# A residual kept in the buffer that the expert scatter adds to, and the second product's evacuation on VectorE

## The reference

```python
x = x + gt1 * (merged @ w_out)
h2 = rmsnorm(x, norm2_g) * (1.0 + sc2) + sh2
x = x + gt2 * moe_ffn(h2, ...)
return rmsnorm(x, final_norm_g)
```

## Time and profile before

| | |
|---|---|
| median of three runs | 3005.07 us |
| profiled execution | 3009.68 us, span 3008.0 us |
| TensorE matmul busy | 2689.5 us (89%) |
| VectorE busy | 1850.1 us (62%) |
| ScalarE busy | 1550.0 us (52%) |
| mean granted TensorE clock | 0.945 of full speed |

### The profile page before, as it was taken

How to read it: one execution, slowest core, us unless ns; L and a number is a source line. 1 busy time by engine, 2 the same in 40 slices (tenths; PEclk the granted TensorE clock), 3 DMA queues, 4 the chain that set the end, 5 groups by cost and what they waited for, 6 DMA issues and landing times. The chain is left out here.

```text
span 3008.0 us, 42817 instructions
## 1 busy us (share of the span) xinstructions
PE 2689.5 (89%) x12623; PEld 2152.7 (72%) x12624; DVE 1850.1 (62%) x2747; ACT 1550.0 (52%) x2231; POOL 315.1 (10%) x372
## 2 busy tenths in 40 slices
PE   4999798977789659999999999999999999999993
PEld 4888676755667547887878778777887787778771
DVE  4332144445545558667676876787657868776855
ACT  5221143433332258556565865776557858665841
POOL 0000010100001211011111111111111111111100
PEclk7999899997889779999999999999999999999995
DMA  6652221202343369759676996799668969976965
GB/s 242 227 194 74 98 82 64 67 30 87 110 149 140 107 226 323 237 193 316 214 249 214 353 308 196 263 344 299 219 210 264 339 198 356 300 247 212 353 202 199
DMA packets 432873, 639.53 MB, mean 213 GB/s; under 512 B 28035, under 2 KB 348725, under 8 KB 432677
## 3 DMA queue, kind: packets, MB, share of 16 engines
q1 hardware_dynamic: 404192, 563.51, 54.8%
q0 software_dynamic: 27392, 70.92, 8.9%
q10 hardware_dynamic: 1220, 4.21, 0.3%
HBM read 594.32 MB, written 64.73 MB: 219 GB/s over the span
## 5 line engine op out<-in xcount | busy, mean ns | idle before, releaser
L2347 DVE TENSOR_TENSOR e_gu_lo<-gu_raw,e_gu_hi 128x1024 fp32r<-128x1024 f32 x564 | 680.8, 1220 | 176.9 <-ACT e_gu_hi L2223 175.8
L82 PE MATMUL e_pgu<-e_gu_hi,e_x_hi 128*128 128x512 f32 x1568 | 643.8, 411 | 7.2 <-issue 7.2
L84 PE MATMUL e_pgu<-e_gu_hi,e_x_lo 128*128 128x512 f32 x1568 | 615.5, 393 | 0.0
L83 PE MATMUL e_pgu<-e_gu_lo,e_x_hi 128*128 128x512 f32 x1568 | 613.9, 392 | 0.0
L2223 ACT ACTIVATE e_gu_hi<-gu_raw 128x1024 fp32r<-128x1024 f32 x564 | 576.9, 1051 | 36.1 <-SPq L2032 18.3
L84 PEld LDWEIGHTS e_pgu<-e_gu_hi,e_x_lo 128*128 128x128 f32 x1568 | 294.8, 188 | 65.1
L2353 DVE TENSOR_TENSOR e_dn_lo<-dn_raw,e_dn_hi 128x1024 fp32r<-128x1024 f32 x280 | 333.1, 1219 | 10.4 <-ACT e_dn_hi L2229 10.4
L82 PEld LDWEIGHTS e_pgu<-e_gu_hi,e_x_hi 128*128 128x128 f32 x1568 | 295.7, 189 | 53.5 <-issue 7.9
L82 PE MATMUL e_pdn<-e_dn_hi,e_a_hi 128*128 128x512 f32 x784 | 310.0, 395 | 22.6 <-DVE e_a_lo L2381 22.6
L83 PEld LDWEIGHTS e_pgu<-e_gu_lo,e_x_hi 128*128 128x128 f32 x1568 | 296.9, 189 | 46.3
L84 PE MATMUL e_pdn<-e_dn_hi,e_a_lo 128*128 128x512 f32 x784 | 306.9, 391 | 0.0
(11 more groups left out here) (402 smaller groups left out, 4097.4 us busy)
## 6 DMA issues: line engine op xcount, KB each, us to landing
gu_raw<-in_w_gate_up_dram SPq DMA_DIRECT2D x572, 512.0 KB, 5.9
dn_raw<-in_w_down_dram SPq DMA_DIRECT2D x142, 1024.0 KB, 9.1
wada_later<-in_w_ada_dram SPq DMA_DIRECT2D x32, 512.0 KB, 3.8
gu_bias<-hidden_bias SPq DMA_DIRECT2D x42, 256.0 KB, 7.7
win_raw<-in_w_in_dram POOLq DMA_DIRECT2D x5, 2048.0 KB, 10.9
proj_by_token<-out_stage SPq DMA_DIRECT2D x32, 256.0 KB, 2.9
wg_raw<-in_w_in_dram POOLq DMA_DIRECT2D x16, 512.0 KB, 5.1
gates_transposed<-g_stage POOLq DMA_DIRECT2D x32, 256.0 KB, 2.3
```

Of the source, the lines that this page charges most:

```text
L82: pe.matmul(out, a[0], w[0], start=first, stop=False)
L83: pe.matmul(out, a[0], w[1], start=False, stop=False)
L84: return pe.matmul(out, a[1], w[0], start=False, stop=last)
L2347: dve.tensor_tensor(gu_lo[:, b, 2 * j:2 * j + 2], gu_raw[:, b, 2 * j:2 * j + 2].rearrange("p k g n -> p k (g n)"), gu_hi[:, b, 2 * j:2 * j ...
```

## The change

Three edits that belong together. `phase_out` stores the residual to the buffer that the scatter adds to (renamed `residual_sum`), the eight zero fills are gone, and only the 128 rows for padding are still filled. `evacuate` moves from ScalarE to VectorE and multiplies by gate2 as well, in one scalar_tensor_tensor; on VectorE it stands behind `low_a` of the second unit, behind the round's last pieces, and behind the last `low_a`. `phase_combine` loads one tile instead of two, multiplies the bias rows by gate2 once, and adds once per tile; its TensorE waits for the gated bias rows, and then for the addition, which is now the only one.

```diff
@@ phase_out, SP
                 if t == 0:
                     sp.wait_ge(zeroed, 1)
-                sp.dma_start(m.y_sum[rows, :].rearrange("p (a n) -> p a n", a=4), zeros).then_inc(zero_out, 16)
-                if t == 0:
                     sp.dma_start(m.y_sum[SEQ:SEQ + P, :].rearrange("p (a n) -> p a n", a=4), zeros).then_inc(zero_out, 16)
                 sp.wait_ge(added, t + 1)
-                sp.dma_start(m.x2[rows, :], x2[:, t % 2]).then_inc(stored[t % 2], 16)
+                sp.dma_start(m.y_sum[rows, :], x2[:, t % 2]).then_inc(stored[t % 2], 16)
...
-            sp.wait_ge(zero_out, 16 * (NT + 1))
+            sp.wait_ge(zero_out, 16)
@@ phase_experts, ScalarE
-            def evacuate(n, s, blocks, kept):
-
-                act.wait_ge(dn_done, n + 3)
-                act.wait_ge(scattered, 16 * blocks + 16)
-                act.wait_ge(dest_kept, kept)
-                act.activation(ys[:], p_dn[:, s], ACT.Copy, scale=dest[:, 0, s, 1:2].bitcast(F32)).then_inc(y_out, 1)
...
-                B = act.snap(U // 4)
...
-                    if l == 1:
-                        after_first(act, r, 0, lambda: evacuate(n - 2, 0, B - 1, 2 * r))
...
-                if two:
-                    evacuate(n - 1, 1, B, 2 * r + 2)
...
-            evacuate(total - 1, 0, act.snap(total // 4) - 1, 2 * n)
@@ phase_experts, VectorE
+            def evacuate(n, s, blocks, kept):
+
+                dve.wait_ge(dn_done, n + 3)
+                dve.wait_ge(scattered, 16 * blocks + 16)
+                dve.wait_ge(dest_kept, kept)
+                dve.scalar_tensor_tensor(out=ys[:], in0=p_dn[:, s], scalar=dest[:, 0, s, 1:2].bitcast(F32), in1=m.gate2[:], op0=ALU.mult,
+                                         op1=ALU.mult).then_inc(y_out, 1)
...
+                B = dve.snap(U // 4)
...
+                    if l == 1:
+                        after_first(dve, r, 0, lambda: evacuate(n - 2, 0, B - 1, 2 * r))
                     while todo:
                         piece()
+                if two:
+                    evacuate(n - 1, 1, B, 2 * r + 2)
...
             low_a(total - 1)
+            evacuate(total - 1, 0, dve.snap(total // 4) - 1, 2 * n)
@@ phase_combine
-                sp.dma_start(x2[:, b], m.x2[t * P:(t + 1) * P, :]).then_inc(y_in[b], 16)
...
-            pe.wait_ge(once_in, 32)
+            pe.wait_ge(gated, 1)
             for t in range(NT):
                 if t >= 2:
-                    pe.wait_ge(summed, t - 1)
+                    pe.wait_ge(x3, t - 1)
...
             dve.wait_ge(once_in, 32)
+            dve.tensor_tensor(bd[:], bd[:], m.gate2[0:NE], ALU.mult).then_inc(gated, 1)
...
-                dve.tensor_tensor(acc[:, b], y[:, b], ps[:, b], ALU.add).then_inc(summed, 1)
-                dve.wait_ge(summed, t + 1)
-                dve.tensor_tensor(acc[:, b], acc[:, b], m.gate2[:], ALU.mult).then_inc(gated, 1)
-                dve.wait_ge(gated, t + 1)
-                dve.tensor_tensor(acc[:, b], acc[:, b], x2[:, b], ALU.add).then_inc(x3, 1)
+                dve.tensor_tensor(acc[:, b], y[:, b], ps[:, b], ALU.add).then_inc(x3, 1)
```

More of the change, by code:

```diff
@@ L2449, in phase_combine @@
         y = sb(ctx, "c_y", [P, 2, D], F32)
-        x2 = sb(ctx, "c_x2", [P, 2, D], F32)
         bd = sb(ctx, "c_bd", [NE, D], F32)
@@ L2460, in phase_combine @@
         biased = sem("c_biased")
-        summed = sem("c_summed")
         gated = sem("c_gated")
@@ L2504, in _ @@
             dve.wait_ge(once_in, 32)
+            dve.tensor_tensor(bd[:], bd[:], m.gate2[0:NE], ALU.mult).then_inc(gated, 1)
             for t in range(NT):
                 b = t % 2
-                dve.wait_ge(y_in[b], 32 * (t // 2 + 1))
+                dve.wait_ge(y_in[b], 16 * (t // 2 + 1))
                 dve.wait_ge(biased, t + 1)
@@ L2554, in build @@
         m.lrT = dram("low_rank_transposed", [RANK, SEQ])
-        m.x2 = dram("residual", [SEQ, D])
         m.h2 = dram("ffn_input", [SEQ, D])
@@ L2558, in build @@
         m.hidden_bias = dram("hidden_bias", [NE, 2 * FF])
-        m.y_sum = dram("expert_sum", [SEQ + P, D])
+        m.y_sum = dram("residual_sum", [SEQ + P, D])
         PASSED[:] = [nc.alloc_semaphore("passed")]
```

## The result

| | before | after |
|---|---|---|
| median of ten runs each, same chip | 3006.66 us (3000.21 to 3014.84) | 3023.2 us (3019.41 to 3030.96) |
| ratio after / before | | 1.0054 [1.0042, 1.0066] |
| profiled execution | 3009.68 us | 3030.51 us |
| VectorE busy | 1850.1 us | 1890.9 us |
| ScalarE busy | 1550.0 us | 1500.4 us |

The change costs 16.5 us of the median where 6.2 were forecast. The time lies 0.2 us above the upper end of the range (by the ratio, on the 3005.07 from which the forecast starts, it is 3021.3, inside by 1.7); "slower by over 0.3%", to which I gave 0.35, happened, not the likeliest case.

A forecast was written before the change was run, and what follows sets the result against it. TensorE was taken to bound the expert stage (busy 1757 of 1840 us, clock granted in full). Terms 12.2 - 3.6 + 7.8 + 2.8 - 13.0 = +6.2 gave 3015.9 us profiled, median 3011.3; range 3000 to 3023.

The forecast's parts named there:

- The evacuation itself: Each evacuation on VectorE from PSUM: 1.29 us, taken from the same operation reading SBUF; ScalarE's takes 1.12.
- Slot 0 (+12.2): Second unit of each round: evacuation behind e_a_lo delays TensorE's first second product 0.30 to 0.40 us; +12.2 us, bounds 9.8 and 15.
- Slot 1 (-3.6): End of two-slot rounds: ScalarE starts its next round earlier, TensorE's wait for e_a_lo shrinks 0.28 us; -3.6 us over 13 rounds.
- The scatter (+7.8): After two-slot rounds: slot 1's scatter starts 2.66 us later, so slot 0's evacuation waits for the single e_y buffer; +7.8 us.
- rival A: Slower: slot 1's scatters land at 11.4 us, so waits at two-slot boundaries cost 24.7 us, not 7.8; time 3028, chance 0.18.
- rival C: Same: scatters land before VectorE reaches the next evacuation, so none waits; the 7.8 goes, time 3003.5, chance 0.06.
- The end of the expert stage (+2.8): Last evacuation, waiting for a scatter: that scatter starts 2.66 us later and the evacuation is 0.17 longer; +2.8 us.
- The last stage (-13.0): Last stage: one addition per tile, 3.47 us per tile, 14.0 us less, with 1.0 added for stores; -13.0 us.
- rival D: Last stage bound by stores at 7.9 us for two tiles, about 4.4 us per tile; +11.7, time 3017, chance 0.10.
- The stage that writes the residual (0): Residual's stage: dropping eight zero fills and storing to the other buffer changes nothing; 0, bounds -1 and +1 us.
- Rival B: Faster: expert stage takes nothing for moved evacuations because existing waits swallow the delays; -13.8 us, time 2991, chance 0.10.

The follow-up runs named there:

- experiment 5: Changed kernel with slot 1's evacuation back on ScalarE (routing weight alone, no gate), slot 0's still on VectorE, one e_y buffer: 3011.55 us, ratio 1.0009.
- experiment 3: Changed kernel with an e_y buffer for each slot, the activation written over its input to make room: 3009.45 us, ratio 1.0003.
- experiment 7: Changed kernel with two e_y buffers, slot 0's evacuation right behind the activation, split g1 behind e_a_lo, slot 1's ahead of the last split: 3001.45 us, ratio 0.9977.
- experiment 1: Changed kernel with the residual in its own buffer again, zero fills back, last stage loading two tiles and adding twice: 3033.15 us, ratio 1.0088.
- experiment 8: Changed kernel with ScalarE evacuating at its old places into two e_y buffers, GpSimd multiplying by the gate before each scatter: 3022.07 us, ratio 1.004.
- experiment 2: Changed kernel with the evacuation back on ScalarE at its old places, routing weight alone, gate left out: 2995.61 us, ratio 0.9956.
- experiment 6: Changed kernel with two e_y buffers, slot 0's evacuation behind the activation, a split between it and e_a_lo, slot 1's ahead of the last split: 3014.69 us, ratio 1.002.
- experiment 4: Changed kernel with one e_y buffer and slot 1's evacuation ahead of the round's last split on VectorE: 3010.55 us, ratio 1.0011.

## Why the prediction was wrong in size and right in mechanism

Three steps failed: slot 0's term leaves out how TensorE restarts behind a wait, the scatter's landing was taken over from another place in the round, and the granted clock was taken as fixed. By term:

**The evacuation itself** (1.29 us): right. All 49 take 1.28.

**Slot 0 (+12.2).** The place was right, the size too small. TensorE's first second product slips by 0.35 as reckoned, but the round grows by 0.48 (40.35 to 40.83), and the runs with this step alone (experiment 5) give 34 x 0.48 = 16.3. The 0.12 to 0.13 on top is for the most part in TensorE's restart: I counted 0.14 between a VectorE end and a matmul start (it is 0.06 here), but the matmul behind the first one comes late too, 0.34 us after it (2022.48 and 2022.82 in the timeline above), where in an unhindered row they start 0.23 apart (at 2012.60 and 2012.83 in the kernel before). That is 0.11 of it, and it is so in every round after. +4.4 over 34 rounds, and with it the part is 16.6, outside my bound of 15. This restart is a term that the prediction left out. That ScalarE delivers earlier and VectorE's queue holds the extra 1.2 us proved right: VectorE's fill alone delayed nothing (experiments 3 and 7).

**Slot 1 (-3.6).** Right: TensorE's wait for e_a_lo ahead of the next round's first second product shrinks from 0.45 to 0.16 us, by 0.29 where 0.28 was forecast.

**The scatter (+7.8).** The start of slot 1's scatter moved by 2.65 us (2.66 forecast), and VectorE then waits for it at 10 boundaries (9 forecast), 11.0 us in all (21.8 less the last 10.8) instead of 7.8. The step that failed is the landing taken over from the trace before: started 2.65 us later it takes 10.54 us in the mean and not 10.08. That is the direction of rival A with under half of its size (A had 11.4 us and 24.7 in all). The rule of the Trainium skill, "DMA: Bandwidth & Descriptors" (section "Anatomy of one DMA — SWDGE (gpsimd) path"), which I named with rival C, is far from the trace here also: not one of 49 lands in under 6.3 us.

**The clock (up to +7 in the profiled execution).** In no term. I read the granted clock (1.00) as a property of the stage. Behind a TensorE wait of some 2 us the lower level (0.51) can follow for 3.4 us. By the rows, eight matmuls start 0.20 later each, 1.6 us a time; by the comparison with experiment 1 it is 1.6 to 1.8. Three of the four falls in the kernel after stand behind the new waits for e_y. The one at 1287 stands behind the wait without a name, which was there before: it is 1.83 us before and 1.90 in experiment 8, without a fall; 1.84 after and 2.20, 2.04 and 1.90 in experiments 2, 6 and 7, with one; 1.57 to 1.63 in experiments 1, 3, 4 and 5, which have no fall in the stage at all. Experiment 6 has a second fall, behind 2.06 us for e_a_lo, and experiment 8 has one, behind 1.99 us for ScalarE's e_y. So the waits with a fall behind them have their length in common (1.79 to 2.20 us) and not what they are for, and the length alone does not decide.

The profiled execution (3030.51) is 7.3 us above the median of ten, so the median holds less of this. Experiment 1 speaks for little: its profiled execution has no fall and lies at its own median (3032.71 against 3033.15), and that median less the residual's 9.35 is 3023.8, within 1 us of the median after.

**The end of the expert stage (+2.8):** 1.6; the last evacuation waited 10.8 us and not 11.25.

**The last stage (-13.0):** -14.7. Per tile 3.41 us against 3.47; the first addition 1.0 later behind the last e_y than before, for the bias rows' product (1.21), where 1.3 was forecast. The allowance of 1.0 for the stores was not needed, and rival D falls: with a third less traffic they land in 3.5 us. Which loop binds was a near miss: TensorE's product (waits of 0.70 us and more), not ScalarE's loop.

**The stage that writes the residual (0):** right. -1.85 in the pair of profiles, but 205.5 to 209.1 us in the eight experiments, of which only experiment 1 (207.66) has the fills.

Summed for the expert stage: 12.2 + 4.4 - 3.8 + 11.0 + 1.6 = 25.4; experiment 1 shows 26.4, the kernel after 33.5 with the clock's 7.1. 33.5 - 14.7 - 1.85 + 3.9 (unchanged code in front) are the 20.8 between the profiled executions. Of the median's 10.3 us beyond the forecast the restart, the waits, the stage's end and the last stage account for 4.4 + 3.2 - 1.2 - 1.7 = 4.7; that leaves some 5.6. 3.0 of them are the base: all sums are against the profiled execution of before, which lies 3.0 above the median of its ten. The cause of the last 2.6 is open. The clock is one candidate, by experiment 1 a weak one; the unchanged code in front is another, which takes 879.8 to 885.6 us in the ten profiles.

Rival B (nothing taken) falls by the waits above; rival A was the nearer neighbour: in the profiled execution scatter waits and clock together are 11.0 + 7.1 = 18.1 us, between my 7.8 and A's 24.7, and only the first is A's mechanism. That the forecast came within 12 us of the time owes something to luck: the last stage gave 1.7 us more and the end of the expert stage 1.2 less than forecast, against 7.6 of underestimate. Rival C falls, since 10 of 13 boundaries wait.

## What to carry to other kernels

An evacuation that moves to the engine which also feeds the bound engine becomes a serial step, however empty that engine is on average; put it in the gap in front of the feed, not behind it (here, with the second buffer and slot 1's earlier place, the ratio to the kernel before goes from 1.0054 to 0.9977). With a buffer of one place, each later producer can become a wait for a DMA landing: allow for another landing time at the new place, since here it changed with it. Price a new wait of TensorE higher than the wait that the profile lists, by the slower restart and, with waits of about 2 us as here, by the clock that may fall behind it.

## What the runs showed of the hardware that I had not expected

- TensorE's clock at its lower level (0.51 granted) for 3.4 us behind single waits of 1.8 to 2.0 us, in some executions: behind 1.84, 1.95, 1.79 and 1.99 us in the kernel after, but not behind 2.44 in the same execution nor behind 2.04 and 2.12 in experiment 1. Over all runs, falls stood behind waits for VectorE, for ScalarE and behind one whose cause the profile does not name.
- A wait that the profile lists as 0.18 us on TensorE lengthens a round by 0.48. The row counts from the end of the product before, 0.39 us behind its start, while unhindered products start 0.23 apart; so the product slipped by 0.34 to 0.35, and the second product behind the wait starts 0.34 instead of 0.23 us after the first.
- The same scatter of 512 KB lands in 9.48, 10.08 or 10.54 us in the mean in three kernels that issue it at three places of the round (9.5 to 10.9 over all runs), and its instruction on GpSimd takes 1.80, 2.11 or 2.19 us.
- GpSimd's multiply of two SBUF tiles (128x1024, float32) takes 2.33 to 2.78 us, and a VectorE subtraction with two SBUF inputs that meets it takes up to 3.06 us instead of 1.22 (3.45 in other rounds).
